# A two-layer model on one core: expert weights awaited in halves, the gate rows in one room, and the last sum of the expert stage closed one pair later

## The reference, cut to what matters

```
x = x + gt1 * mix                      # gt1: the layer's gate row 2
h = modulate(rms_norm(x, norm2_g[l]), sh2, sc2)
# hier_moe: the best of 4 groups, then the best 2 of its 8 experts, for each token
hid = silu(xb @ w1[e]) * (xb @ w3[e])  # w1[e], w3[e]: 1024 x 512
ys  = (hid @ w2[e]) * w_b[:, None]     # w2[e]: 512 x 1024
out = zeros((T, D)).at[buf_tok].add(ys)
x = x + gt2 * ffn                      # gt2: the layer's gate row 5
return rms_norm(x, final_g)            # after the second layer
```

## Time and profile before

| what | value |
|---|---|
| median of 3 runs | 2286.8 us (2283.88 to 2288.28) |
| profiled execution, its own time | 2283.03 us |
| its span, first to last instruction | 2281.2 us |
| granted TensorE clock, mean | 0.998 |
| TensorE busy | 2249.4 us, 99% |
| VectorE, ScalarE, GpSimd busy | 1057.5, 461.1, 74.4 us |
| DMA, hardware queue | 649.45 MB, 69.2% of 16 engines' span |
| expert stage, layer 0 and layer 1 | about 1105 to 1545 us, and 1833 to 2274 us |

### The profile page before, as it was taken

One profiled execution on the slowest core, in us unless ns is written; L12 is line 12 of the kernel. 1 busy time (PEld: TensorE's weight loads), 2 busy tenths in 40 slices (PEclk: granted clock), 3 DMA queues, 4 the chain that ended last, 5 costly groups with the idle time before them and its releaser, 6 DMA issues.

```text
span 2281.2 us, 26770 instructions
## 1 busy us (share of the span) xinstructions
PE 2249.4 (99%) x11302; PEld 1377.5 (60%) x11302; DVE 1057.5 (46%) x2098; ACT 461.1 (20%) x1041; POOL 74.4 (3%) x131
## 2 busy tenths in 40 slices
PE   9999999999999999999999999999999999999998
PEld 6569547886497459997533433335999743333343
DVE  4578756668588567675311111125767421111122
ACT  3411003358111011230211111101122021111111
POOL 2000000010000000000000000000000000000000
PEclk9999999999999999999999999999999999999999
DMA  7378725354689515246999999995424899999997
GB/s 296 116 313 358 309 76 202 149 184 162 246 346 407 181 54 211 98 185 256 410 427 428 428 427 427 427 419 210 175 78 168 344 426 427 427 427 428 427 427 285
DMA packets 59318, 672.52 MB, mean 295 GB/s; under 512 B 7521, under 2 KB 7809, under 8 KB 18865
## 3 DMA queue, kind: packets, MB, share of 16 engines
q1 hardware_dynamic: 51888, 649.45, 69.2%
q0 software_dynamic: 7296, 21.21, 2.7%
HBM read 667.37 MB, written 3.26 MB: 294 GB/s over the span
## 4 chain that ended last, share of the span: by engine, by line
PE 89%; DMA 7%; DVE 3%; issue 0%; POOL 0%; ACT 0%; SPq 0%; DVEq 0%; POOLq 0%; ACTq 0%
PE ps L101 86%; DMA ring<-in_exp_w 5%; DVE arena L114 1%; DVE arena L117 1%; PE ps L350 1%; DMA arena<-ssm_rows 1%; PE ps L3112 1%; DMA ring<-in_ada_w 0%; PE ps L639 0%; DMA ring<-in_attn_w_in 0%; PE ps L2139 0%; DVE X L117 0%; DVE arena L110 0%; PE ps L1328 0%; POOL small L117 0%
## 5 line engine op out<-in xcount | busy, mean ns | idle before, releaser
L101 PE MATMUL ps<-arena 128*64 128x512 f32 (+5 forms) x4612 | 1075.9, 446 | 12.6 <-DVE arena L117 4.6
L101 PEld LDWEIGHTS ps<-arena 128*128 128x128 f32 (+2 forms) x4612 | 536.5, 168 | 425.3 <-issue 393.5
L101 PE MATMUL ps<-ring,arena 128*64 128x512 f32 (+2 forms) x1592 | 501.8, 583 | 1.5 <-DMA ring<-in_exp_w 1.5
L101 PE MATMUL ps<-XTGB,ring 128*128 128x256 f32 (+1 forms) x2032 | 382.5, 344 | 0.0
L101 PEld LDWEIGHTS ps<-XTGB,ring 128*128 128x128 f32 x2032 | 333.5, 191 | 43.8 <-issue 9.5
L101 PEld LDWEIGHTS ps<-ring,arena 128*64 128x64 f32 (+1 forms) x1592 | 185.0, 151 | 240.7 <-issue 236.4
L122 DVE COPY arena<-ps 128x512 f32<-128x512 f32 (+5 forms) x133 | 63.3, 496 | 401.1 <-PE ps L101 282.3
L121 ACT COPY arena<-ps 128x512 f32<-128x512 f32 (+3 forms) x187 | 85.0, 473 | 690.2 <-PE ps L101 283.6
L117 DVE TENSOR_TENSOR arena<-ps,arena 128x256 f32<-128x256 f32 (+5 forms) x290 | 127.1, 475 | 119.1 <-PE ps L101 89.0
L101 PE MATMUL ps<-XTGB,arena 128*128 128x128 f32 (+2 forms) x736 | 178.4, 396 | 0.0
L101 PE MATMUL ps<-ring,XTGB 128*128 128x512 f32 (+3 forms) x484 | 166.4, 498 | 1.9 <-DMA ring<-in_attn_w_in 1.8
(11 more groups left out here) (162 smaller groups left out, 1050.6 us busy)
## 6 DMA issues: line engine op xcount, KB each, us to landing
arena<-in_exp_w SPq DMA_DIRECT2D x96, 2048.0 KB, 28.9
ring<-in_exp_w SPq DMA_DIRECT2D x64, 2048.0 KB, 28.0
ring<-in_mlp_w SPq DMA_DIRECT2D x25, 2048.0 KB, 11.4
ring<-in_ada_w SPq DMA_DIRECT2D x20, 2048.0 KB, 9.5
XTGB<-in_exp_w SPq DMA_DIRECT2D x16, 2048.0 KB, 28.5
ring<-in_ssm_w_in SPq DMA_DIRECT2D x12, 2048.0 KB, 8.2
ring<-in_w_in SPq DMA_DIRECT2D x12, 2048.0 KB, 8.0
ring<-in_gate_w SPq DMA_DIRECT2D x12, 2048.0 KB, 7.9
```

The costliest lines, as they stand in the source:

```text
L101: return self.e.matmul(o, lhsT=lhsT, rhs=rhs, start=start, stop=stop, skip_group_check=True)
```

## The change

Four things are changed, all in the second block.

- From pair 4 on (`HALVES`), a pair's w1, w3 and w2 are loaded by `chunk_halves`: the first halves of both slabs (8 KB a partition), then the second halves, which have semaphores of their own (`ringh`). TensorE waits for the second halves in the middle of `inner` and `outer`. Pair 15's w3 and w2 are loaded as before. Pairs 0 to 3 are too.
- `GATE[2]` and `GATE[5]` share one room. Gate row 5 is loaded by `moe_pool` after the mixer's last use of gate row 2. The place NRING + 5 is lent from the time at which the `xbase` places are, ahead of `out_w`.
- `LAST` is (3, 7, 11, 14): pair 14 is summed up in the fourth group, which is closed and scattered within pair 15. Only pair 15 goes straight to the tokens.
- `final_g` keeps its room, now called `FINAL`, at the arena's top, and waits, as before, for the last tenant of NRING + 5.

```diff
+        def chunk_halves(sp, keys, name, offs, kc, n):
+            for h in range(2):
+                for key, off in zip(keys, offs):
+                    if h == 0:
+                        i, was = ring.take(key)
+                        if was is not None:
+                            sp.wait_ge(at("free", was))
+                        shape[key] = (kc, n)
+                    i = ring.home[key]
+                    f = slice(h * SLAB // 2, (h + 1) * SLAB // 2)
+                    src = d[name][off:off + P * SLAB].rearrange("(p f) -> p f", p=P)
+                    sp.landed(sp.e.dma_start(ring.bufs[i][:, f], src[:, f]), f"ringh{i}" if h else f"ring{i}",
                               ("w half" if h else "w", key))
...
-        GATE = {2: arena.ap[:, ASZ - D:ASZ], 5: arena.get(D)}
+        gate_row = arena.get(D)
+        GATE = {2: gate_row, 5: gate_row}
+        FINAL = arena.ap[:, ASZ - D:ASZ]
...
-            for i in (2, 5):
-                gate_rows(pool, 0, i)
+            gate_rows(pool, 0, 2)
...
+            ring.tenant[NRING + 5] = ("extra", l)
+            ring.turn.append(NRING + 5)
             for n in range(2):
                 slab(sp, ("ow", l, n), "out_w", (l * 2 + n) * P * SLAB, 8, 512)
...
-        LAST = (3, 7, 11, 13)
+        LAST = (3, 7, 11, 14)
+        HALVES = 4
...
-            for j, until in ((5, "gate row"), (2, "router")):
-                ring.tenant[NRING + j] = (until, l)
-                ring.turn.append(NRING + j)
+            ring.tenant[NRING + 2] = ("router", l)
+            ring.turn.append(NRING + 2)
...
+                    elif i >= HALVES and (k == 0 or i < NP - 1):
+                        chunk_halves(sp, keys, nm, offs, kc, n)
...
+            gate_rows(pool, l, 5, at("free", ("gate row", l)))
             pool.wait_ge(at("rows", nn - 1, 0), at("rows", nn - 1, 1))
...
-                    if c == 4 and i == NP - 1 and nm == "exp_w3":
+                    if c == 4 and i >= HALVES:
                         pe.wait_ge(at("w half", (nm, l, i, 0)), at("w half", (nm, l, i, 1)))
...
+                        if f == 2 and i >= HALVES:
+                            pe.wait_ge(at("w half", ("exp_w2", l, i, 0)), at("w half", ("exp_w2", l, i, 1)))
...
-                        to_tokens(*((i, 1, (0, 1)) if n else (i - 1, 1, (0, 1))))
+                        if n:
+                            to_tokens(i, 1, (0, 1))
...
-                if i == NP - 2:
+                if i == NP - 1:
                     for n in range(2):
                         combine(i - 1, n)
-                    scatter(NG - 1)
+                    scatter(NG - 1, (0,))
                 inner(i, "exp_w3")
...
-                else:
-                    to_tokens(i - 1, 0, (0,))
+                else:
+                    scatter(NG - 1, (1,), (0,))
                 turn_h(i)
```

More of the change, by code:

```diff
@@ L223, in build @@
         for i in range(NRING + 7):
+            sems[f"ringh{i}"] = ctx.enter_context(nc.semaphore(f"s_ringh{i}"))
             sems[f"ring{i}"] = ctx.enter_context(nc.semaphore(f"s_ring{i}"))
@@ L271, in slabs_in_halves @@
                     sp.landed(sp.e.dma_start(o, src), f"half{sem + j}" if h else f"ring{place[key]}",
+                              ("w half" if h else "w", key))
+        def chunk_halves(sp, keys, name, offs, kc, n):
[10 more added lines that the diff above has]
+                    sp.landed(sp.e.dma_start(ring.bufs[i][:, f], src[:, f]), f"ringh{i}" if h else f"ring{i}",
                               ("w half" if h else "w", key))
@@ L2753, in mix_pool @@
             if l:
-                gate_rows(pool, 1, 2, at("free", last_over_gate[0]))
-                gate_rows(pool, 1, 5, at("xy ready", 0, NP - 1, 1))
+                gate_rows(pool, 1, 2, at("xy ready", 0, NP - 1, 1))
                 pool.wait_ge(at("free", last_over_mask[0]))
@@ L2989, in av_done @@
         def av_done(l, t):
-            return [at("sum", l, NG + 1, t, n) for n in range(2)]
+            return [at("sum", l, NG, t, n) for n in range(2)]
         def moe_sp(sp, l):
-            for j, until in ((5, "gate row"), (2, "router")):
-                ring.tenant[NRING + j] = (until, l)
-                ring.turn.append(NRING + j)
+            ring.tenant[NRING + 2] = ("router", l)
+            ring.turn.append(NRING + 2)
             ring.turn.append(NRING + 6)
@@ L3028, in moe_pool @@
                 pool.wait_ge(at("free", last_over_gate[l]))
-                pool.landed(pool.e.dma_start(GATE[2], bcast(d["final_g"][0:1, :])), "gb", ("gb", "final"))
+                pool.landed(pool.e.dma_start(FINAL, bcast(d["final_g"][0:1, :])), "gb", ("gb", "final"))
             general(pool, l, flag_reg(pool, l), general_pool)
@@ L3149, in combine, with scatter @@
                             ("xc", l, i, n))
-            def scatter(g):
-                for n in range(2):
+            def scatter(g, ns=(0, 1), ts_=(0, 1)):
+                for n in ns:
                     pe.wait_ge(at("pgt ready", l, g), at("yg", l, g, n))
-                    for t in range(2):
+                    for t in ts_:
                         ps = bank(pe, "xo", l, g, t, n)
@@ L3160, in to_tokens @@
             def to_tokens(i, n, ts_):
-                g = NG + i - (NP - 2)
+                g = NG
                 pe.wait_ge(at("pwt ready", l, i), at("xy ready", l, i, n))
@@ L3211, in moe_pe @@
                     gather(1, 4)
-                elif i < NP - 2:
+                elif i < NP - 1:
                     combine(i - 1, 1)
-                elif i == NP - 2:
-                    gather(i + 1, 4)
-                else:
-                    to_tokens(i - 1, 0, (1,))
-                if 1 <= i < NP - 2:
+                else:
+                    scatter(NG - 1, (1,), (1,))
+                if 1 <= i < NP - 1:
                     gather(i + 1, 0)
@@ L3349, in weights_turned @@
                 if i in ptok:
-                    if i == NP - 1:
-                        v.wait_ge(at("xc", l, i - 2, 1))
+                    v.wait_ge(at("pgt", l, NG - 1), at("gcw", l, NG - 1))
                     v.then_inc(v.cp(ptok[i], ps_of("pw", l, i)[:, 0:T]), ("pwt ready", l, i), ("read", "pw", l, i))
@@ L3401, in to_tokens @@
                     v.then_inc(v.tt(o, o, ps, ALU.add), ("sum", l, g, t, n), ("read", "xo", l, g, t, n),
-                               *([("moe end", l)] if g == NG + 1 else []))
+                               *([("moe end", l)] if g == NG else []))
             def rows_out(i, n):
@@ L3407, in rows_out @@
                 v.wait_ge(at("xy", l, i, n))
-                if i == NP - 1:
-                    v.wait_ge(at("xo", l, NG, 1, n))
-                elif i - 1 in LAST:
+                if i - 1 in LAST:
                     v.wait_ge(at("xo", l, LAST.index(i - 1), 1, n))
@@ L3441, in moe_dve @@
                     group_turned(i // 4)
-                if i == NP - 2:
+                if i == NP - 1:
                     for n in range(2):
                         group_sum(NG - 1, n)
-                    for n in range(2):
-                        to_tokens(NG - 1, n)
+                    to_tokens(NG - 1, 0)
                 v.wait_ge(at("silu", l, i), at("exp_w3", l, i))
@@ L3464, in moe_dve @@
                     group_places(i // 4 + 1)
+            to_tokens(NG - 1, 1)
+            rows_out(NP - 1, 0)
             to_tokens(NG, 0)
-            rows_out(NP - 1, 0)
+            rows_out(NP - 1, 1)
             to_tokens(NG, 1)
-            to_tokens(NG + 1, 0)
-            rows_out(NP - 1, 1)
-            to_tokens(NG + 1, 1)
             if l == 0:
```

8 lines of the change are left out of this document (3 added, 5 removed).

## The result

| | before | changed |
|---|---|---|
| median of 7 runs each | 2285.57 us (2281.96 to 2288.28) | 2293.15 us (2290.63 to 2295.65) |
| ratio to before, 95% interval | 1 | 1.0034 (1.0022 to 1.0046) |
| span of the profiled execution | 2281.2 us | 2290.9 us |

The kernel became slower by 7.6 us in the medians (5.0 to 10.5 by the interval), and by 9.7 us between the two profiled executions. The forecast was +2.0.

A forecast was written before the change was run, and what follows sets the result against it. The full DMA was taken as the bound, pair 15's landing and the work behind it setting the end. Layer 0 +1.6 us and layer 1 +0.4 made +2.0 on the 2286.8 median: 2288.8 us, range 2281 to 2295.

The forecast's parts named there:

- the dearer halves: Weight slabs from pair 4 on: halves cost more than their rows behind pair 0, up to 2294.6 us; chance 19%.
- slower sides: Rivals in which halves cost more, the tail gives nothing or the queue starves; chance 27% together.
- Start: Ahead of each layer's full DMA stretch: gap filled (-2.0 us), gate row 5 loaded there (1.2 us); together -0.8 us.
- Rate: Slabs from pair 4 through pair 15's w1: 68 in 8 KB rows cost 3.9 us a layer, bounds 0 to 6.8.
- The second rival: Weight slabs from pair 4 on: halves cost 0.08 to 0.10 us a slab, sum +5.0 to +7.8 us; chance 19%.
- price per packet: Weight loads: about 3 cycles (3.5 ns) a packet, 0.028 us a slab, 1.9 us a layer; sum would be -2.0 us.
- Tail: Pair 15, behind the last landing: TensorE waits for w2's second half, less work follows; -1.5 us a layer, bounds 0 to -2.5.
- the cover: End of layer 1: `final_g`, issued after `outer(15)`, lands after 4.3 us, 0.4 us before it is wanted.

The follow-up runs named there:

- kernel with every second partition: Changed kernel, each half being every second partition (64 rows of 16 KB a DMA), both awaited before the product; one run, 2289.19 us.
- kept-warm kernel: Changed kernel plus four idle matmuls on TensorE behind layer 0's expert stage; 2297.25 us, ratio 1.0053 to the kernel before.
- 64 neighbouring partitions: Changed kernel, each half being 64 neighbouring partitions with 16 KB rows, both awaited before the product; 2974.04 us, ratio 1.3017 to the kernel before.

## Why the prediction was off in size

The measured time lies in the stated range, near its upper end, and the range reached so far only because the dearer halves were taken in; the forecast's own spread (2284 to 2292) does not hold it. The difference of 7.6 us is above the 4.6 that the forecast called noise, so what came is one of its slower sides (27%).

**Start: right.** Forecast -0.8 a layer. The gap is filled, and the last half behind pair 0 lands 1.1 us earlier, 0.5 of it from before the stage (`out_w` is issued 0.5 earlier): -0.6. The traces scatter by 2 us in when `out_w` is issued in layer 0, but not in what follows: from there to that half it is 86.1 to 86.6 us in both layers of every kernel with the gate rows in one room, and 86.7 to 87.3 in the others.

**Rate: the term that was mis-sized.** The mechanism was right, the DMA full at a lower rate and all of it on the path. The term was +3.9 a layer, from 0.046 to 0.07 us a slab; it measured 5.9 (0.087) here, and 5.4 (0.080) over all traces. The low end of the forecast did not compare like with like: it set six halves without a longer spacing (2.483) against the mean of 77 slabs with some (4.921). Against the median of those slabs (4.897) the same halves give 0.07, as the windows before did, and the middle between 0.046 and 0.07 was too low from the start. The longer spacings make the rest. The windows after, 428 to 421, are 0.081 a slab.

The second rival's range is 0.08 to 0.10 us a slab (2291.8 to 2294.6), and the time fell into it, but not by that rival's reason. It read 5.0 us a slab from pair 15's w3 halves, from times rounded to 0.1 us; the trace has 1523.96 - 1514.02 = 9.94 us for the four, 4.97 a slab, as behind pair 0. So nothing here shows that halves cost more in a long queue. Two layers make +4.0 us of the 7.7 by which the profiled difference (9.7) exceeds the forecast one (2.0).

The forecast weighed a price per packet from the Trainium skill (DMA: Bandwidth & Descriptors, "Why small descriptors are slow (HBM only)"), estimated at 0.028 us a slab. With 8 more rows on each of 16 engines the measured 0.087 is 11 ns a row, three times that estimate. That rows and not DMAs carry it is shown by the kernel with every second partition (427 GB/s); its full stretch takes 379.7 and 379.8 us in the two layers, as with whole slabs.

**Tail: right in kind.** Forecast -1.5, measured -1.1: TensorE waits for w2's second column half, as said, and the work behind it takes 5.72 us instead of 5.3. The forecast had halves pay for the four matmuls between w1 and w3, and the table above bears it out: with halves at the last pairs the later closing takes 0.9 off, and 0.3 is the halves' alone; without them it adds 1.8 to 2.5.

**`final_g`: the cover failed.** The 1.2 us out of layer 1's stretch are there: from the slabs behind pair 0 to the last landing layer 1 lost 4.8 us, layer 0 5.9, though this stretch scatters by as much from trace to trace. In whole slabs it shows better: to pair 15's w1 the two layers with `final_g` in between take 380.3 and 380.4 us, those without 378.7 to 379.9. But the load took from 2279.26 to 2284.8, 5.5 us and not 4.3, with the DMA otherwise done (3.7 to 5.5 over the kernels here that load it at the end), and came 1.25 us late instead of 0.4 early. The forecast called this cover thin; its bound was 2.5. Moving the load away took the wait away.

**Not foreseen: the start of layer 1.** 1.6 us: 0.34 of idle time more, and 1.2 from the clock. TensorE idles between the layers in every kernel here. Behind it the granted clock is at 1.2 GHz for a while, in the kernel before for 3 us, in the changed one for 7 (windows of before, then of after; the first row of each is at 0.5):

```profile
1549.00:1552.00 3.00, 2.87 (x9) 1.93 (x9) 1.43 (x5) 1.51 (x4) 0.00 (x0) 0.50 0.69 295
1552.00:1559.00 7.00, 7.00 (x17) 3.04 (x16) 1.34 (x1) 0.00 (x0) 3.09 (x4) 0.99 0.59 219
```

```profile
1552.00:1559.00 7.00, 6.22 (x14) 3.43 (x15) 2.76 (x6) 1.80 (x6) 2.56 (x3) 0.51 0.55 231
1559.00:1565.00 6.00, 6.00 (x16) 2.80 (x15) 0.00 (x0) 0.00 (x0) 0.00 (x0) 1.00 0.58 214
```

That the clock makes the product longer is shown by the kept-warm kernel. Why it stays down 3 us in one kernel and 7 in the other is open: the first product took 13.8 to 15.2 us over the kernels here (13.17 where matmuls ran ahead), each profiled once, and the one attempt to hold the clock failed.

**The sum again.** +2.0 forecast, +4.0 rate, +0.8 tail, +1.25 `final_g`, +1.6 layer 1's start, +0.4 start of the stretches, -0.5 upstream: +9.6 of the 9.7 between the profiled executions. The runs' medians lie 7.6 apart; one execution can differ from the median by the 2 us between them.

## What to carry to other kernels

Where the DMA is full for hundreds of microseconds, what a smaller row costs has to be read like for like, median against median or a long stretch against a long stretch, and not from a few landings against a mean, since a difference of 0.04 us a slab, times the slabs, is the whole result. Halve loads only where the consumer waits for them, here the last three pairs. An edit that shortens the work behind the last landing (closing the group later) is worth something only if the work ahead of that landing still fits before it: here it took 0.9 us a layer off the work behind the landing with halves, and added 1.8 to 2.5 without.

## What was not expected of the hardware

- 64 neighbouring partitions: 213 GB/s; every second partition: 427, with the same rows and bytes. A row's packet took 1240 ns instead of 615, with all 16 DMA engines as busy (a share of 1.01).
- With 8 KB rows SyncE's own issue took 2.13 us in the full stretch, where whole slabs took 0.33 (pair 15's second w1 slab) and the DMAs of every second partition, with 16 KB rows, 0.60 (median). With few loads ahead of them halves of 8 KB took 0.33 to 0.44. The DMA stayed full, so it cost nothing here.
- A 512 KB broadcast on GpSimd's queue took 5.5 us to land with the weights' queue empty, and 3.7 to 5.5 over the kernels that load `final_g` at the end.
